# First stage of a 512-token two-block network: half the chunk turns on each partition half, tables copied across, other orders of loads, sines, copies and products

## The chip, the cores and the metric

The kernel runs on one core of a Trainium2 chip. The core has five engines that run side by side, each through its own list of instructions in order: TensorE (PE, matrix products and transposes), VectorE (DVE), ScalarE (ACT), GpSimd (POOL) and SyncE (SP), which here only issues transfers (DMA). They wait for each other through semaphores. The metric is the time of one execution on the device in microseconds (us); lower is better.

## What is computed

A network of a first block (two layers: a diagonal state-space mixer "S5", then sparse attention, each with a gated MLP) and a second block (four kinds of attention, cross attention into 256 memory tokens, an MLP). The change touches only the S5 mixer at the start and the key/value product of the memory tokens that runs beside it:

```python
def s5_mixer(u, lam_re, lam_im, log_dt, b_re, b_im, c_re, c_im, d_skip, w_glu):
    lam = lax.complex(lam_re, lam_im)
    dt = jnp.exp(log_dt)[:, None]
    a_bar = jnp.exp(lam * dt)
    b_bar = ((a_bar - 1.0) / lam)[..., None] * lax.complex(b_re, b_im)
    ug = u.reshape(bsz, length, S5_GROUPS, S5_GROUP)      # 64 groups of 16 channels
    bu = jnp.einsum('blgh,gph->blgp', ug, b_bar)          # 64 complex states per group
    _, states = lax.associative_scan(_ssm_combine, (a_seq, bu), axis=1)
    y = jnp.einsum('blgp,ghp->blgh', states, c).real.reshape(bsz, length, D_MODEL)
    y = y + d_skip * u
    y = jax.nn.gelu(y)
    val, gate = jnp.split(y @ w_glu, 2, axis=-1)
    return val * jax.nn.sigmoid(gate)
```

The input `u` is the RMS-normed `x` (512 tokens of 1024 channels), all in float32.

## The kernel before

The program is one list of instructions for each engine, written out by hand, with semaphores between them. The order on an engine is the order of the code; nothing is scheduled by a tool.

The S5 stage cuts the 512 tokens into 64 chunks of 8 tokens. Inside a chunk the recurrence is a matrix product (the "taps"); from chunk to chunk it is a scan with a real decay, after the states have been turned back by the chunk's angle, and forth again after the scan. For this there are two tables, `tab_c` and `tab_s` (cosine and sine of group times chunk, 128 partitions by 64 groups by 64 chunks). Partitions 0 to 63 hold the real part and 64 to 127 the imaginary part of the same 64 states, so both halves of a table are the same numbers.

Preparation. DVE makes the powers of the transition (`exp_small`, `cmul`), then per block of 8 groups an input map (`input_map(b)`, into `in_w`) and an output map (`output_map(b)`, into `out_a`), and once the angles in turns, reduced to a fraction (`chunk_turns`, three operations over the whole table, lines 1479 to 1481). ACT squares the eight slices of `x` (L799), copies the transposed memory (`memT`, L829), the B and C matrices (`b_s`, `c_n`, `c_s`), scales `x` into `u` (L855, eight slices), and makes the tables (`table(k)`, four quarters, each of a sine, an absolute value and a sine, L890, L891, L893). PE transposes the weights and `u` and computes keys and values of the memory (L2004, L2008).

The loop over eight blocks b of 8 groups. On PE: `s5_rotate_in(b)` (L2060, L2061), `s5_in(b+1)`, `s5_lags(b+1)`, `s5_rotate_out(b)`, `s5_in_turn(b+2)`, `s5_out(b)` (L2018, L2019). On DVE: `rotate_in(b)` (L1518, L1519, the first reader of the tables), `input_map(b+2)`, `scan_chunks(b)`, `output_map(b+2)`. On ACT: `lag_out(b+1)` (L878), `states_out(b)` (L885), `decay_out(b+1)`, `in_map_out(b+2)`, `gelu(b)` (L860). `states_out(b)` feeds `s5_out(b)`. SP copies `lag` to `taps` by eight transfers a block, after `s5_out(b-1)` (semaphore `s5_y`) and `lag_out(b)`; `lag_out(b+1)` waits until the taps of block b have landed, and `s5_out(b)` as well.

Behind the loop comes the gated product with `w_glu` (the GLU, L2121), whose weights pass in slots through `raw`: SP loads a slot by two transfers, ACT rounds it (`round_slot`, L899), POOL makes the rest (`split_rest`, L647). The rounding of slot 0 stands on ACT ahead of the last `states_out`:

```python
            act.wait_ge(s5_v, NB)
            round_slot(0, 0, 1)
            states_out(NB - 1)
```

## Time and profile before

| what | value |
|---|---|
| median of three runs | 1960.52 us (1957.99 to 1961.86) |
| the profiled execution | 1957.8 us |
| its span (first to last instruction) | 1955.9 us |
| granted TensorE clock, mean over the span, as a share of full speed | 0.991 |
| PE busy | 1905.9 us, 97% of the span |
| start of the GLU's matmuls behind the S5 stage | 168.5 us |

The profile gives the start and the length of each instruction, counted from the span's start, and what ended the idle time before it. A matmul's record overlaps the next one, so the distance from one start to the next is its cost. PEclk is the clock granted to TensorE: 1.00 is 2.4 GHz, 0.50 is 1.2 GHz.

### The profile page before, as it was taken

How to read it: one execution, taken by the hardware profiler on the slowest of the kernel's cores; microseconds unless marked ns; L12 is line 12 of the kernel's file. 1: busy time of each engine (PE TensorE's matmuls, PEld its weight loads, DVE VectorE, ACT ScalarE, POOL GpSimd, SP SyncE). 2: the span in 40 equal slices, each digit the busy share in tenths (PEclk: the TensorE clock that was granted, in tenths of full speed). 3: DMA queues.
4: the chain of work that ended last, by engine and by line, in shares of the span. 5: the costliest groups of instructions: out<-in, count | busy, mean ns of one | idle time of the engine just before them, and what ended most of it. 6: DMA issues, size and time to landing. Idle time of an engine off the chain costs nothing.

```text
span 1955.9 us, 24958 instructions
## 1 busy us (share of the span) xinstructions
PE 1905.9 (97%) x9663; PEld 1541.8 (79%) x9663; DVE 749.2 (38%) x1281; ACT 742.2 (38%) x1142; POOL 826.9 (42%) x412
## 2 busy tenths in 40 slices
PE   5999999999999999999999999999999999999998
PEld 4777888888888878767888888888775778888887
DVE  7983231111002378882311110020546657403721
ACT  6634242232223243684423222242457462212212
POOL 1003444444444458654434344444245444343433
PEclk9899999999999899999999999999999999999999
DMA  7114323333322213202333323324220223324231
GB/s 192 27 25 138 99 82 100 93 100 86 103 95 70 83 65 105 68 2 65 87 106 87 105 78 102 115 87 145 76 65 16 83 56 96 108 86 108 86 108 64
DMA packets 209706, 169.26 MB, mean 87 GB/s; under 512 B 19545, under 2 KB 174633, under 8 KB 209560
## 3 DMA queue, kind: packets, MB, share of 16 engines
q1 hardware_dynamic: 207456, 164.61, 28.5%
q10 hardware_dynamic: 2168, 3.52, 0.5%
q8 instruction: 55, 0.90, 0.2%
q14 instruction: 27, 0.22, 0.0%
HBM read 163.10 MB, written 2.65 MB: 85 GB/s over the span
## 4 chain that ended last, share of the span: by engine, by line
PE 89%; ACT 3%; DVE 3%; issue 2%; DMA 1%; POOL 1%; SPq 1%; POOLq 0%; DVEq 0%; ACTq 0%
PE PS L2121 77%; PE PS L2411 2%; PE PS L2402 2%; PE PS L2421 2%; DMA xp<-in_x 1%; PE PS L2018 1%; PE PS L2019 1%; PE PS L2194 1%; DVE taken L1884 1%; PE PS L2364 0%; ACT probs_t L1188 0%; PE PS L2039 0%; SPq L494 0%; PE PS L2051 0%; ACT junk L799 0%
## 5 line engine op out<-in xcount | busy, mean ns | idle before, releaser
L647 POOL TENSOR_TENSOR w_lo<-raw,w_hi 128x2048 fp32r<-128x2048 f32 x145 | 670.5, 4624 | 960.7 <-ACT w_hi L899 837.5
L899 ACT ACTIVATE w_hi<-raw 128x2048 fp32r<-128x2048 f32 x145 | 277.8, 1916 | 629.6 <-PE PS L2121 629.6
L2121 PE MATMUL PS<-xT_hi,w_hi 128*128 128x512 f32 (+1 forms) x1152 | 441.0, 383 | 1.5 <-DVE xT_lo L1568 1.1
L2121 PE MATMUL PS<-xT_lo,w_hi 128*128 128x512 f32 (+1 forms) x1152 | 438.2, 380 | 0.0
L2121 PE MATMUL PS<-xT_hi,w_lo 128*128 128x512 f32 (+1 forms) x1152 | 438.0, 380 | 0.0
L2121 PEld LDWEIGHTS PS<-xT_hi,w_hi 128*128 128x128 f32 x1152 | 216.6, 188 | 47.4 <-issue 6.7
L2121 PEld LDWEIGHTS PS<-xT_lo,w_hi 128*128 128x128 f32 x1152 | 216.6, 188 | 41.5
L2121 PEld LDWEIGHTS PS<-xT_hi,w_lo 128*128 128x128 f32 x1152 | 216.7, 188 | 40.5
L2121 PE MATMUL PS<-w_hi,hT_hi 128*128 128x512 f32 x608 | 236.9, 390 | 0.0
L2121 PE MATMUL PS<-w_hi,hT_lo 128*128 128x512 f32 x608 | 236.6, 389 | 0.0
L2121 PE MATMUL PS<-w_lo,hT_hi 128*128 128x512 f32 x608 | 236.5, 389 | 0.0
L2121 PE MATMUL PS<-w_hi,xT_hi 128*128 128x512 f32 (+2 forms) x592 | 231.9, 392 | 0.7 <-ACT ki_raw L1102 0.7
L2121 PE MATMUL PS<-w_hi,xT_lo 128*128 128x512 f32 (+2 forms) x592 | 228.6, 386 | 0.0
L2121 PE MATMUL PS<-w_lo,xT_hi 128*128 128x512 f32 (+2 forms) x592 | 228.4, 386 | 0.0
L1637 DVE TENSOR_TENSOR x_res<-x_res,PS 128x512 f32<-128x512 f32 x40 | 27.4, 686 | 397.3 <-PE PS L2121 397.3
L1654 DVE TENSOR_TENSOR gbuf<-gbuf,PS 128x512 f32<-128x512 f32 x44 | 30.3, 688 | 378.4 <-PE PS L2121 378.4
L2121 PEld LDWEIGHTS PS<-w_hi,xT_hi 128*128 128x128 f32 x592 | 114.0, 193 | 28.8 <-issue 8.5
L2121 PEld LDWEIGHTS PS<-w_lo,hT_hi 128*128 128x128 f32 x608 | 114.1, 188 | 23.7
L2121 PEld LDWEIGHTS PS<-w_hi,hT_lo 128*128 128x128 f32 x608 | 114.1, 188 | 23.6
L2121 PEld LDWEIGHTS PS<-w_hi,hT_hi 128*128 128x128 f32 x608 | 114.1, 188 | 23.6
L2121 PEld LDWEIGHTS PS<-w_hi,xT_lo 128*128 128x128 f32 x592 | 114.2, 193 | 21.4
L2121 PEld LDWEIGHTS PS<-w_lo,xT_hi 128*128 128x128 f32 x592 | 114.3, 193 | 19.9
(335 smaller groups left out, 2024.7 us busy)
## 6 DMA issues: line engine op xcount, KB each, us to landing
raw<-in_ffn_w_gate_up SPq DMA_DIRECT2D x88, 512.0 KB, 4.5
raw<-in_ffn_w_down SPq DMA_DIRECT2D x40, 512.0 KB, 4.3
raw<-in_w_up SPq DMA_DIRECT2D x32, 512.0 KB, 5.1
raw<-in_w_down SPq DMA_DIRECT2D x32, 512.0 KB, 4.3
raw<-in_dsa_w_in SPq DMA_DIRECT2D x28, 512.0 KB, 4.4
raw<-in_w_in SPq DMA_DIRECT2D x21, 512.0 KB, 4.4
raw<-in_s_w_glu SPq DMA_DIRECT2D x16, 512.0 KB, 4.5
raw<-in_dsa_w_o SPq DMA_DIRECT2D x8, 512.0 KB, 4.7
```

Of the source, the lines that this page charges most:

```text
L647: pool.tensor_tensor(w_lo[:, par, :], raw[:, par, :], f32(w_hi[:, par, :]), ALU.subtract).then_inc(w_split, 1)
L899: act.activation(w_hi[:, par, :], raw[:, par, :], ACT.Copy).then_inc(w_rounded, 1)
L1637: tt(x_res[:, tb, cols], x_res[:, tb, cols], PS[:, 4 + tb, :], ALU.add).then_inc(n_free, 1)
L1654: tt(gbuf[:, pair, 1, :], gbuf[:, pair, 0, :], PS[:, 2 * pair + 1, :], ALU.mult).then_inc(t_free, 1)
L1884: tt(lg[:, :, 0:cols - 1], lg[:, :, 0:cols - 1], rest[:, :, 1:cols], ALU.mult).then_inc(st_prob, 1)
L2018: mm(o, uT[:, GB * b + g, :], taps[:, g, :, :].rearrange("p t h -> p (t h)"), start=True, stop=False)
L2019: ins = mm(o, states[:, g, :], out_a[b % 3][:, g, 1:CH + 1, :].rearrange("p t h -> p (t h)"), start=False, stop=True)
L2121: ins = mm(o, a if weights_stay else c, c if weights_stay else a, start=first and n == 0, stop=last and n == 2)
L2194: ins = tr(PS[:, banks[4 * (tb // 2) + i], at:at + P], x_n[:, tb, P * k:P * k + P], ident[:, :])
L2402: mm(PS[:, dot_bank(u0, t), 0:k.shape[1]], q[half:half + HD], k[half:half + HD], start=True, stop=True).then_inc(col_dot, 1)
L2411: ins = tr(PS[:, 4 + e % 2, P * j:P * j + P], probs[:, e % ring, P * j:P * j + P], ident[:, :])
L2421: ins = mm(PS[HD * i:HD * i + HD, 6 + (p // 4) % 2, at:at + P], units[2 * p + i][3][j], probs_t[:, 2 * (p % 2) + i, P * j:P * j + P], star ...
```

## The change

- The angles in turns are made for half of the groups on each partition half (`turns`, in `raw`, groups 0 to 31 on partitions 0 to 63, the others on 64 to 127). `table(n)` makes a quarter of the tables on one partition half; SP copies it to the other half by two transfers (`table_copy`).
- On ACT `table(0)` stands behind `lag_out(0)`, `table(1)` behind `in_map_out(1)`, `table(2)` behind `lag_out(1)` and `table(3)` behind `lag_out(2)`, the last one behind the first GELU.
- ACT's first activation is a sine; the two small sines stand ahead of the copies of B. The swapped `b_s` is copied after four squares, three squares stand behind `c_s`. The rsqrt of `x` is made in halves. The copy of the keys stands in the middle of the `u` slices.
- The row of `norm_mix` is loaded once (4 KB) and spread over the partitions by a product with ones, where it was loaded 128 times (512 KB). `log_dt` is loaded first, and the first exponential waits for it alone.
- PE makes the swap of B right behind the memory's transposes, and the values in two parts, the second behind `s5_lags(0)`. The transposes of `u` go to the banks in another order.
- Slot 0 of `w_glu` is loaded behind the taps of all eight blocks, where it was loaded behind the keys.

```diff
@@ table of turns
-        turns_i = place("turns_i", "arena", 48 * KB, [P, G, NC], I32)
+        turns_i = place("turns_i", "w_lo", 0, [P, G // 2, NC], I32)
+        turns = place("turns", "raw", 0, [P, G // 2, NC])
@@ SP, the loads
+            sp.dma_start(small[:, 0, :], w["s5_log_dt"][0:1, :].broadcast_to([P, G])).then_inc(ld_dt, 16)
...
-            sp.dma_start(small[:, 0, :], w["s5_log_dt"][0:1, :].broadcast_to([P, G])).then_inc(ld_lam, 16)
+            sp.dma_start(g_row[:, :], w["norm_mix"][0:1, :]).then_inc(ld_rows, 16)
...
-            sp.dma_start(g_row[:, :], w["norm_mix"][0:1, :].broadcast_to([P, D])).then_inc(ld_rows, 16)
@@ SP, the GLU's first slot
-                    else:
-                        sp.wait_ge(kv_done, g + 1)
-                    v = raw[:, g % 2, :].rearrange("p (k t n) -> p k t n", t=2, n=256)
-                    put(g % 2, v[:, :, 0, :], glu[:, k:k + 4, 256 * j:256 * j + 256])
-                    put(g % 2, v[:, :, 1, :], glu[:, k:k + 4, D + 256 * j:D + 256 * j + 256])
                     if g == 0:
+                        def table_copy(n):
+                            side, gs = n // 2, slice(G // TABS * n, G // TABS * n + G // TABS)
+                            of, to = slice(GP * side, GP * side + GP), slice(GP - GP * side, P - GP * side)
+                            sp.wait_ge(s5_cos, 2 * n + 2)
+                            sp.dma_start(tab_s[to, gs, :], tab_s[of, gs, :]).then_inc(s5_tab[n], 16)
+                            sp.dma_start(tab_c[to, gs, :], tab_c[of, gs, :]).then_inc(s5_tab[n], 16)
...
+                            if b == 0:
+                                table_copy(0)
+                                table_copy(1)
+                                sp.wait_ge(kv_sb, 2)
+                                sp.dma_start(kv_dram, kv_new[:, :, :]).then_inc(kv_out, 16)
+                            if b == 1:
+                                table_copy(2)
+                                table_copy(3)
+                    v = raw[:, g % 2, :].rearrange("p (k t n) -> p k t n", t=2, n=256)
+                    put(g % 2, v[:, :, 0, :], glu[:, k:k + 4, 256 * j:256 * j + 256])
+                    put(g % 2, v[:, :, 1, :], glu[:, k:k + 4, D + 256 * j:D + 256 * j + 256])
@@ ACT
-            act.activation(warm[:, :], sign[:, :], ACT.Copy)
+            act.activation(warm[:, :], sign[:, :], ACT.Sin)
...
-            def table(k):
-                gs = slice(G // TABS * k, G // TABS * (k + 1))
+            def table(n):
+                side, at = n // 2, G // TABS * (n % 2)
+                rows, gs, of = slice(GP * side, GP * side + GP), slice(G // TABS * n, G // TABS * n + G // TABS), slice(at, at + G // TABS)
                 act.wait_ge(s5_turns, 1)
...
-            kv_copy(0)
-            kv_copy(1)
             in_map_out(0)
             lag_out(0)
+            table(0)
+            kv_copy(1)
             for q in range(8):
...
             decay_out(0)
-            table(0)
             in_map_out(1)
-            for k in range(1, TABS):
-                table(k)
+            table(1)
             for b in range(NB - 1):
                 lag_out(b + 1)
+                if b < 2:
+                    table(2 + b)
                 states_out(b)
@@ DVE
-            dve.wait_ge(ld_lam, 16 * 5)
+            dve.wait_ge(ld_dt, 16)
+            exp_small(pt(3), pt(0), pt(4), pt(5), pt(6))
             dve.wait_ge(ld_const, 16 * 2)
             dve.wait_ge(s5_nat_sb, 1)
-            exp_small(pt(3), pt(0), pt(4), pt(5), pt(6))
...
                 if b % 2 == 0:
-                    dve.wait_ge(s5_cos, b + 2)
+                    dve.wait_ge(s5_tab[b // 2], 32)
```

Three places show how the lists change. ACT before, from the last quarter of the tables into the loop (y is the GELU's output, ACT_TABLE_LOAD the change of the function tables between sine and GELU):

```order
L890 ACTIVATE tab_s<-tab_c 128x1024
L891 ACTIVATE tab_c<-tab_c 128x1024
L893 ACTIVATE tab_c<-tab_c,quarter 128x1024
L878 ACTIVATE lag<-PS 16x1024
L885 ACTIVATE states<-PS 128x512
L866 ACTIVATE decay<-r 128x8x63
L872 ACTIVATE in_t<-PS 128x1024
L860 ACT_TABLE_LOAD
L860 ACTIVATE y<-PS 64x8x8x16
L878 ACTIVATE lag<-PS 16x1024
L885 ACTIVATE states<-PS 128x512
```

ACT of the change, from the same `lag_out(1)` on:

```order
L899 ACTIVATE lag<-PS 16x1024
L914 ACTIVATE tab_s<-turns 64x1024
L915 ACTIVATE turns<-turns 64x1024
L917 ACTIVATE tab_c<-turns,quarter 64x1024
L906 ACTIVATE states<-PS 128x512
L887 ACTIVATE decay<-r 128x8x63
L893 ACTIVATE in_t<-PS 128x1024
L881 ACT_TABLE_LOAD
L881 ACTIVATE y<-PS 64x8x8x16
L899 ACTIVATE lag<-PS 16x1024
L914 ACT_TABLE_LOAD
L914 ACTIVATE tab_s<-turns 64x1024
```

Before, no table work stands between `lag` and `states`. Now a quarter stands there in blocks 0 and 1, the second one with a change of function tables ahead; its other two operations and then `states` follow.

SP before, with the waits, from the first load of `w_glu` on:

```order
L454 DMA raw<-in_s_w_glu 128x4x256 [waits kv_done]
L454 DMA raw<-in_s_w_glu 128x4x256
L487 DMA kv_dram<-kv_new 128x1024 [waits kv_sb]
L494 DMA taps<-lag 16x1024 [waits s5_lag_sb,s5_zero]
L494 DMA taps<-lag 16x8x112
L494 DMA taps<-lag 16x8x96
```

SP of the change, the same place and then the end of the last block's taps:

```order
L499 DMA taps<-lag 16x8x32
L499 DMA taps<-lag 16x8x16
L490 DMA tab_s<-tab_s 64x1024 [waits s5_cos]
L491 DMA tab_c<-tab_c 64x1024
L490 DMA tab_s<-tab_s 64x1024 [waits s5_cos]
L491 DMA tab_c<-tab_c 64x1024
L505 DMA kv_dram<-kv_new 128x1024 [waits kv_sb]
```

```order
L499 DMA taps<-lag 16x8x64
L499 DMA taps<-lag 16x8x48
L499 DMA taps<-lag 16x8x32
L499 DMA taps<-lag 16x8x16
L458 DMA raw<-in_s_w_glu 128x4x256 x4
L515 DMA x_res<-in_x 128x4x1024 [waits s5_gelu]
```

The load of slot 0 has moved from ahead of the first taps to behind the last ones, where it now stands together with slot 1 (four transfers); the first table copies stand behind the eight taps transfers of block 0.

## Rows read from the trace of the kernel before

**Rows 1.** The page, part 1: busy time by engine.

```profile
PE 1905.9 (97%) x9663; PEld 1541.8 (79%) x9663; DVE 749.2 (38%) x1281; ACT 742.2 (38%) x1142; POOL 826.9 (42%) x412
```

**Rows 2.** Timeline of DVE up to the loop: start, us, what, idle before.

```profile
8.19 0.20 DVE L1391 TENSOR_SCALAR small<-small 128x64 f32<-128x64 f32 x1 [5.55 <-ACT small L802]
...
18.47 0.22 DVE L1416 TENSOR_TENSOR small<-small 128x64 f32<-128x64 f32 x1 [1.62 <-ACT small L812]
...
47.33 4.42 DVE L1479 TENSOR_TENSOR tab_c<-small,rot 128x4096 f32<-128x4096 f32 x1 [0.24 <-ACT u L855]
...
54.12 4.42 DVE L1481 TENSOR_TENSOR tab_c<-tab_c,turns_i 128x4096 f32<-128x4096 f32 x1
...
66.57 0.69 DVE L1518 TENSOR_TENSOR v<-PS,tab_c 128x512 f32<-128x512 f32 x1
```

**Rows 3.** Timeline of ACT up to the loop.

```profile
16.74 1.28 ACT L811 ACT_TABLE_LOAD   x1
...
24.18 1.06 ACT L799 ACTIVATE junk<-xp 64x1024 f32<-64x1024 f32 x1 [1.60 <-DMA xp<-in_x]
...
38.87 8.43 ACT L855 ACTIVATE u<-xp,rstd 64x1024 f32<-64x1024 f32 x8
...
60.77 1.05 ACT L890 ACTIVATE tab_s<-tab_c 128x1024 f32<-128x1024 f32 x1
...
62.79 1.15 ACT L893 ACTIVATE tab_c<-tab_c,quarter 128x1024 f32<-128x1024 f32 x1
```

**Rows 4.** SP's issues and their landing: the taps (64 issues) and `kv_dram`.

```profile
L494 SPq DMA_DIRECT2D taps<-lag x64: 559/600/1822, 53.7 to 160.9; - x64
DMA to landing us min/median/max: 1.8/2.2/3.4
...
kv_dram<-kv_new SPq DMA_DIRECT2D x1, 512.0 KB, 2.7
```

**Rows 5.** Timeline of PE in the loop's blocks 0 and 1.

```profile
67.92 2.07 PE L2060 MATMUL PS<-v,ident 128*128 128x512 f32 x2 [2.12 <-DVE v L1519]
...
78.61 0.43 PE L2018 MATMUL PS<-taps,uT 128*64 128x128 f32 x2
...
82.25 1.12 PE L2060 MATMUL PS<-v,ident 128*128 128x512 f32 x2
...
90.75 0.43 PE L2018 MATMUL PS<-taps,uT 128*64 128x128 f32 x2
```

**Rows 6.** Timeline of ACT in block 1.

```profile
88.76 1.01 ACT L878 ACTIVATE lag<-PS 16x1024 f32<-16x1024 f32 x1 [5.39 <-DMA taps<-lag]
89.99 0.60 ACT L885 ACTIVATE states<-PS 128x512 f32<-128x512 f32 x1 [0.21 <-PE PS L2069]
```

**Rows 7.** Timeline of ACT, SP and PE at the end of the loop.

```profile
156.37 1.02 ACT L860 ACTIVATE y<-PS 64x1024 f32<-64x1024 f32 x1 [4.25 <-PE PS L2019]
157.29 1.90 ACT L899 ACTIVATE w_hi<-raw 128x2048 fp32r<-128x2048 f32 x1
159.94 0.60 ACT L885 ACTIVATE states<-PS 128x512 f32<-128x512 f32 x1 [0.75 <-PE PS L2069]
...
161.52 1.14 SPq L454 DMA_DIRECT2D raw<-in_s_w_glu  x2
...
162.76 0.40 PE L2018 MATMUL PS<-taps,uT 128*64 128x128 f32 x2 [2.22 <-issue]
...
166.37 2.23 PE L2097 MATMUL PS<-ident,y 64*128 64x64 f32 x32
168.53 0.50 PE L2121 MATMUL PS<-w_hi,xT_hi 128*128 128x512 f32 x1
```

**Rows 8.** What the transfers moved from 161.4 to 167.0 us, in 40 slices.

```profile
GB/s 14 75 29 0 0 39 20 0 0 0 102 146 168 256 366 300 366 329 307 380 395 329 366 351 380 373 380 388 380 388 395 293 205 117 29 0 0 0 0 0
```

**Rows 9.** Stretches of PE: us, length, busy (x), PEclk, DMA share, GB/s.

```profile
55.00:55.50 0.50, 0.50 (x11) 0.83 0.61 98
...
72.00:72.50 0.50, 0.50 (x5) 0.61 0.00 0
...
1948.00:1949.00 1.00, 0.88 (x4) 1.00 0.06 25
...
1953.00:1954.00 1.00, 0.00 (x0) 0.57 0.29 115
```

More of the change, by code:

```diff
@@ L39 @@
 TABS = 4
+TURN_BANKS = [4, 5, 6, 0, 1, 2, 3, 7]
 HD = 64
@@ L640, in _ @@
             rsqrt(rstd[:, 32:34], ssq[:, 32:34], 2, 1.0 / D).then_inc(mem_rstd, 1)
-            pool.wait_ge(s5_sq, CH)
-            rsqrt(rstd[0:NC, 0:CH], ssq[0:NC, 0:CH], CH, 1.0 / D, NC).then_inc(s5_rstd, 1)
+            for half in range(2):
+                rows = slice(CH // 2 * half, CH // 2 * half + CH // 2)
+                pool.wait_ge(s5_sq, rows.stop)
+                rsqrt(rstd[0:NC, rows], ssq[0:NC, rows], CH // 2, 1.0 / D, NC).then_inc(s5_rstd, 1)
             def split_rest(g, par):
@@ L802, in _ @@
             act.activation(small[:, 1:3, :].rearrange("p a g -> p (a g)"), PS[:, 0, 0:2 * G], ACT.Copy).then_inc(s5_nat_sb, 1)
+            act.wait_ge(s5_ang, 1)
+            act.activation(small[:, 12, :], small[:, 11, :], ACT.Sin).then_inc(s5_sin, 1)
+            act.activation(small[:, 13, :], small[:, 11, :], ACT.Sin, scale=0.5).then_inc(s5_sin, 1)
             act.wait_ge(s5_nat, 2)
@@ L1472, in _ @@
             link(ts(pt(5).bitcast(I32), pt(11), cycles, None, ALU.mult))
-            link(stt(pt(10), pt(5).bitcast(I32), -1.0, pt(10), ALU.mult, ALU.add))
+            for side in range(2):
+                rows, gs = slice(GP * side, GP * side + GP), slice(G // 2 * side, G // 2 * side + G // 2)
+                link(stt(small[rows, 13, 0:G // 2], small[rows, 5, gs].bitcast(I32), -1.0, small[rows, 10, gs], ALU.mult, ALU.add))
             def chunk_turns():
-                dve.wait_ge(s5_u, CH)
+                dve.wait_ge(kv_done, 1)
                 dve.wait_ge(ld_rot, 16)
-                link(tt(tab_c[:, :, :], pt(10).unsqueeze(2).broadcast_to([P, G, NC]), rot[:, 3 * P:3 * P + NC].unsqueeze(1).broadcast_to([P, G, NC]), ALU.mult))
-                link(ts(turns_i[:, :, :], tab_c[:, :, :], 1.0, None, ALU.mult))
-                tt(tab_c[:, :, :], tab_c[:, :, :], turns_i[:, :, :], ALU.subtract).then_inc(s5_turns, 1)
+                link(tt(turns[:, :, :], small[:, 13, 0:G // 2].unsqueeze(2).broadcast_to([P, G // 2, NC]),
+                        rot[:, 3 * P:3 * P + NC].unsqueeze(1).broadcast_to([P, G // 2, NC]), ALU.mult))
+                link(ts(turns_i[:, :, :], turns[:, :, :], 1.0, None, ALU.mult))
+                tt(turns[:, :, :], turns[:, :, :], turns_i[:, :, :], ALU.subtract).then_inc(s5_turns, 1)
             def over_k(ap, b, n):
@@ L1975, in _ @@
             tr(PS[:, 0, 0:len(GAINS) * KT], gain_rows[:, :], ident[0:len(GAINS) * KT, 0:len(GAINS) * KT]).then_inc(gains_t, 1)
+            pe.wait_ge(ld_rows, 16)
+            pe.wait_ge(const_set, 1)
+            for b in range(2):
+                ins = mm(PS[:, 5 + b, :], ones[0:1, :], g_row[:, 512 * b:512 * b + 512], start=True, stop=True)
+            ins.then_inc(s5_grow, 1)
             pe.wait_ge(s5_nat_sb, 3)
@@ L1983, in _ @@
                     ins.then_inc(mem_t, 1)
+            pe.wait_ge(s5_bn, 1)
+            pe.wait_ge(ld_rot, 16)
+            pe.wait_ge(gains_sb, 1)
+            for b in range(2):
+                ins = mm(PS[:, 7 * b, :], rot[:, 2 * P:3 * P], b_n[:, 32 * b:32 * b + 32, :].rearrange("p g h -> p (g h)"), start=True, stop=True)
+            ins.then_inc(s5_swap, 1)
             pe.wait_ge(ld_c, 16 * 3)
```

106 lines of the change are left out of this document (52 added, 54 removed).

## The prediction

> **What bounds the kernel now.** I read the page first. PE is busy for 97% of the span [rows 1], and behind the first stage nothing in the lists changes; so the question is when PE starts the GLU's matmuls, 168.5 us before [rows 7], and everything behind moves with that. Then I read the timelines of the first stage engine by engine. Up to the loop the start is set by ACT and DVE in turn: `x` lands at 24.2, ACT then works without a pause until the last slice of `u` at 47.3 (38.87 + 8.43) [rows 3], only then may DVE make the turns, which take from 47.33 to 58.54, and after the two maps of block 1 it reaches the first `rotate_in` at 66.57 [rows 2]. The loop is bound by PE: one round, from 67.92 on, has matmuls back to back, and rounds are about 12.2 us long (78.61 to 90.75) [rows 5]. But PE waits for ACT's `states` at the end of each round, and ACT reaches it only just in time: in block 1 `lag` waits for the taps' landing, starts at 88.76, and `states` starts 0.2 us behind its end [rows 6]. So anything put between `lag` and `states` lands on the path. The loop's end is also tight: slot 0 is rounded at 157.29, long after its load, `states` follows at 159.94, and the last `s5_out` starts at 162.76 when the last taps land [rows 7].
>
> **Part 1, up to the loop.** `x` is issued behind one small transfer more (0.6 us), and the 512 KB broadcast stood behind it in the queue; I take its landing as 0.3 us later. From there to the end of `u` ACT has the same work as before (23.1 us, 24.18 to 47.30) plus one copy of 512 columns (0.6, as `states` [rows 6]) in the middle: 24.5 + 23.7 = 48.2. I see no wait in it, since the swap on PE stands earlier than before. Then `in_map_out(0)` and `lag_out(0)`, 1.0 each as `lag` [rows 6]: 50.1. `table(0)` has 1024 elements a partition as before, only on 64 partitions; a quarter took 3.17 (60.77 to 63.94) [rows 3]. If time goes by elements per partition it is 3.2 again, and it ends at 53.3. Halving the partitions gains ACT nothing.
>
> DVE gains twice. The first exponential (fourteen operations of about 0.25, 3.5 us) now fits into the 5.55 us in which DVE waited, and the 1.62 us wait for the small sines loses the table load of 1.28 [rows 2, 3]: about 4.6 us together. So the first input and output maps end near 42 instead of 47.1, the turns cost half of 11.2 (5.6) and end at 47.7, and the maps of block 1 (58.54 to 66.57 before, 8.0 with two small memsets) end at 55.7 [rows 2]. All of this is ahead of ACT, so DVE waits.
>
> SP issues the eight taps transfers of block 0 behind `lag`, from 50.1, 0.64 us each: 55.2. Then the two copies of `table(0)`, 256 KB each, the second issued at 55.8. No such copy is in the trace. The nearest row is `kv_dram`, 512 KB from SBUF in 2.7 us [rows 4]; from below the shortest taps landing, 1.8, from above the 4.5 us of a loaded slot (161.5 to 166.0) [rows 8]. I take 2.9, nearest to `kv_dram`: the table is there at 58.7, and `rotate_in(0)` starts at about 58.8 where it was 66.57. **Minus 7.8** (bounds -8.9 and -6.2). PE has its part (`u`, `s5_in(0)`) done by 58 even at half clock.
>
> **Part 2, the first two rounds.** From `rotate_in(0)` on DVE to `s5_out(0)` on PE it took 12.0 us (66.57 to 78.61), part of it at 1.2 GHz: the clock fell at 55.3 in the narrow transposes of `u` and rose at 72.2, 4.3 us after PE went back to work at 67.92 [rows 5, 9]. I keep that, so PE is ready at 70.9. Its `lags` of this round end near 68.2; `lag_out(1)` takes 1.0, and then `table(2)` stands ahead of `states_out(0)`: 3.15 + 0.6, so `states` is there at 72.9. Before, the tables were all made by then. **Plus 2.0** (0.5 to 3.2).
>
> In round 1 `table(3)` stands between `lag_out(2)` and `states_out(1)`, behind the first GELU, so the function tables must change back: 1.28 + 3.17 = 4.45 [rows 3]. The slack was 0.2 us [rows 6]. PE needs nothing else and idles: **plus 4.2** (3.1 if the load could run ahead of the wait for `lag`, 4.5 at most). The load back for `gelu(1)` (1.28) lies in ACT's wait for `s5_out(1)`, which is 2 us in every round. `table_copy(2)` and `(3)` are issued behind the taps of block 1 and have two rounds before `rotate_in(4)`: nothing.
>
> The row gives 1.28 us for a change of tables (16.74), and DVE waited 1.62 for it with a sine behind it [rows 2, 3]. The Trainium skill, "ScalarE: Activation LUTs", section "What ACT_TABLE_LOAD costs", counts a drain on top and says about 2.66 us for every switch; by that the sum below would be 1.4 higher. No gap for such a drain stands in this trace ahead of the load, so the rows decide.
>
> After round 1 the loop stands at -7.8 + 2.0 + 4.2 = -1.6. Rounds 2 to 6 are as before.
>
> **Part 3, the loop's end.** Call T the time when `s5_out(6)` is done, 156.3 before [rows 7]. The last taps are issued from T to T + 5.2, then slot 0. Before, the two transfers issued there (slot 1, 161.52) had landed at 166.0, which is T + 9.7 [rows 7, 8]. Now slot 0 has that place. ACT meets `round_slot(0)` ahead of `states_out(7)`, and cannot pass it: T + 9.8, + 1.9 for rounding, + 0.6 for `states`, so the last `s5_out` starts at T + 12.3 instead of T + 6.4. **Plus 5.9** (4.9 with a landing 1 us sooner; 8.9 if slots 0 and 1, now issued together, share the bandwidth). Behind this `s5_out` stand on PE the turns of `y` and the GLU; POOL's split of slot 0 (4.6 us, beside `s5_out`) and slot 1 are ready before PE asks.
>
> PE idles about 8.4 us there. At the end of the trace the clock fell to 0.50 at 1953.1, 4.3 us after the last matmul at 1948.9 [rows 9]; an idle time of 2.2 us ahead of 162.76 cost nothing. So PE resumes at 1.2 GHz, and if it needs 4.3 us again, half of that is lost: **plus 2.1** (0 if it stays high; 5.8 if `s5_out` and the turns, 3.6 + 2.2 us, run wholly at half speed).
>
> **Sum.** -7.8 + 2.0 + 4.2 + 5.9 + 2.1 = +6.4 us. The profiled execution took 1957.8 (span 1955.9), so its counterpart is 1964.2. It lies 2.7 below the median of the runs; against the median 1960.5 I predict **1966.9**. A difference under 0.2% (3.9 us) can't be told from no change.
>
> **Rivals.**
> - *The clock stays at 2.4 GHz.* If PE's denser work before 60 us keeps the clock up, `s5_out(0)` comes 2.2 us earlier (half of the 4.3 us), and if the idle time at the end doesn't lower it, 2.1 more: +2.1, 1962.6, not to be told from no change. For it: PE now works with fewer pauses before the loop. Against it: the narrow transposes of `u`, in which it fell, are still there, and an idle time of 4.3 us did lower it. It decides at both places together. Chance 0.13.
> - *More is lost.* The 4.1 us idle time in round 1 is as long as the one after which the clock fell, which would cost another 2.1; or slot 0 lands with slot 1, up to 3.0. +8.5 to +9.5, about 1969.5. Chance 0.17. The Trainium skill, "TensorE: Matmul & The Clock Gate", Part 1, lets the clock fall after an idle stretch and rise only after sustained work, which speaks for this rival; the trace agrees at its end.
> - *`x` lands earlier.* If the broadcast took bandwidth from `x` (B, the memory and `x` are 3.9 MB from about 7 to 24.2 us, so 512 KB are 2.3 us by this estimate), everything on ACT up to the loop moves by 2.6: +3.8, 1964.3. Against it: it was issued behind `x`. Chance 0.09.
> - *Faster.* The copies land in 1.8 us, `x` earlier, and the clock high: -1.0 or less. It needs all three. Chance 0.04.
>
> **How the numbers follow.** The forecast has 0.57, its own range +4 to +9 (1964.5 to 1969.5). Slower by over 0.2%: nearly all of it and the second rival, and half of the third, 0.79. Within 0.2%: the first rival, half of the third and the forecast's edge, 0.16. Faster 0.05. The range 1962.0 to 1971.0 takes in the first two rivals.
>
> **What would show it.** `rotate_in(0)` on DVE near 58.8, released by a transfer; a PE wait of 2 us ahead of `s5_out(0)` and of 4 us ahead of `s5_out(1)`, both for ACT's `states`; a table load inside round 1 of 1.28; the rounding of slot 0 at about 164.5, released by a transfer, and the last `s5_out` at 167, with a granted clock of 0.50; the GLU at about 175 instead of 168.5. The prediction is wrong if slot 0 lands much earlier or later than T + 9.7, or if the loop starts more than 1.5 us away from 60.

## The result, and the profile after

The changed kernel takes **1968.57 us** (median of six runs, 1967.32 to 1970.75); the kernel before, run beside it on the same chip, takes 1958.01 us (median of six, 1957.37 to 1961.86). The ratio is 1.0052, with a 95% interval of 1.0039 to 1.0065: slower by 10.6 us. The profiled execution took 1967.32 us (span 1965.5), 9.5 more than the one of before; the difference of the spans is 9.6, and that is what the following rows account for. The page's busy times hardly differ from those of before [rows 1]: PE's is 4.9 higher, DVE's 5.8 lower (the turns over half the elements). So what is lost has to be looked for in PE's waits and in the clock.

```profile
PE 1910.8 (97%) x9667; PEld 1544.9 (79%) x9667; DVE 743.4 (38%) x1282; ACT 742.7 (38%) x1143; POOL 829.1 (42%) x414
```

**Up to the loop.** Timeline of the changed kernel (start, length, what, idle time before it and what ended it): ACT's first slice of `x`, then SP's issues, then DVE's first reader of the tables.

```profile
23.95 1.06 ACT L817 ACTIVATE junk<-xp 64x1024 f32<-64x1024 f32 x1 [3.06 <-DMA xp<-in_x]
...
49.44 5.58 SPq L499 DMA_DIRECT2D taps<-lag  x8
55.06 0.60 SPq L490 DMA_DIRECT2D tab_s<-tab_s  x1
55.70 0.60 SPq L491 DMA_DIRECT2D tab_c<-tab_c  x1
...
59.36 0.69 DVE L1546 TENSOR_TENSOR v<-PS,tab_c 128x512 f32<-128x512 f32 x1 [4.02 <-DMA tab_c<-tab_c]
```

`rotate_in(0)` starts at 59.36 where it was 66.57 [rows 2]: 7.2 us sooner. DVE had nothing to do for 4.02 us there; it was released by the copy of `tab_c` across the partitions, issued at 55.70 behind the eight taps transfers. The copies took this long from issue to landing (minimum, median and maximum of the four of `tab_c`; `tab_s` had 2.9, 2.9 and 3.0):

```profile
DMA to landing us min/median/max: 3.5/3.6/4.0
```

**The first two rounds.** ACT's timeline, then PE's.

```profile
67.94 1.02 ACT L899 ACTIVATE lag<-PS 16x1024 f32<-16x1024 f32 x1 [4.67 <-PE PS L2078]
68.98 1.06 ACT L914 ACTIVATE tab_s<-turns 64x1024 f32<-64x1024 f32 x1
...
72.18 0.60 ACT L906 ACTIVATE states<-PS 128x512 f32<-128x512 f32 x1
...
84.73 1.01 ACT L899 ACTIVATE lag<-PS 16x1024 f32<-16x1024 f32 x1 [5.47 <-DMA taps<-lag]
85.76 1.28 ACT L914 ACT_TABLE_LOAD   x1
87.06 1.05 ACT L914 ACTIVATE tab_s<-turns 64x1024 f32<-64x1024 f32 x1
...
90.25 0.60 ACT L906 ACTIVATE states<-PS 128x512 f32<-128x512 f32 x1
```

```profile
72.83 0.43 PE L2054 MATMUL PS<-taps,uT 128*64 128x128 f32 x2 [2.14 <-ACT states L906]
...
78.14 1.13 PE L2096 MATMUL PS<-v,ident 128*128 128x512 f32 x2
90.90 0.69 PE L2054 MATMUL PS<-taps,uT 128*64 128x128 f32 x2 [4.19 <-ACT states L906]
...
96.18 1.12 PE L2096 MATMUL PS<-v,ident 128*128 128x512 f32 x2
```

Both tables lie between `lag` and `states`, and PE waits for `states` 2.14 and 4.19 us. What the reader should also see are the distances behind these waits: `s5_out(0)` takes 72.83 to 78.14, 5.31 us, and `s5_out(1)` 90.90 to 96.18, 5.28 us, where it took 3.64 before (78.61 to 82.25 [rows 5]). Nothing was added to it; the granted clock is low (below).

**The loop's end.** SP, ACT and PE in the changed kernel.

```profile
158.69 5.08 SPq L499 DMA_DIRECT2D taps<-lag  x8
163.81 2.24 SPq L458 DMA_DIRECT2D raw<-in_s_w_glu  x4
...
158.65 1.02 ACT L881 ACTIVATE y<-PS 64x1024 f32<-64x1024 f32 x1 [4.25 <-PE PS L2055]
169.52 1.91 ACT L923 ACTIVATE w_hi<-raw 128x2048 fp32r<-128x2048 f32 x1 [9.85 <-DMA raw<-in_s_w_glu]
171.34 0.58 ACT L906 ACTIVATE states<-PS 128x512 f32<-128x512 f32 x1
...
171.97 0.69 PE L2054 MATMUL PS<-taps,uT 128*64 128x128 f32 x2 [9.14 <-ACT states L906]
...
177.66 2.23 PE L2135 MATMUL PS<-ident,y 64*128 64x64 f32 x32
179.83 0.50 PE L2159 MATMUL PS<-w_hi,xT_hi 128*128 128x512 f32 x1
```

The four transfers of slots 0 and 1 are issued together behind the last taps, the rounding waits 9.85 us for the first of them, `states` stands behind the rounding, and PE waits 9.14 us. The last `s5_out` takes 5.69 us in place of 3.61 [rows 7], and the GLU starts at 179.83, 11.3 us later than before.

**The clock.** Stretches of PE: start and end, length, busy us of the five engines (instructions), PEclk, DMA share, GB/s. The first six are the changed kernel, where the clock falls and rises (the third and the fourth lie in `s5_out(0)` and `s5_out(1)`); the last stands much later, in the index products of the sparse attention, which the change does not touch.

```profile
53.00:54.00 1.00, 1.00 (x9) 0.88 (x10) 0.96 (x2) 1.00 (x3) 0.00 (x0) 0.67 0.37 63
63.00:64.00 1.00, 1.00 (x4) 0.34 (x2) 0.96 (x2) 0.27 (x1) 0.00 (x0) 0.71 0.00 0
...
74.00:75.00 1.00, 1.00 (x7) 1.00 (x6) 0.97 (x2) 0.98 (x2) 0.00 (x0) 0.50 0.00 0
92.00:93.00 1.00, 1.00 (x7) 1.00 (x6) 0.00 (x0) 0.98 (x2) 0.00 (x0) 0.50 1.08 229
...
166.00:167.00 1.00, 0.00 (x0) 0.00 (x0) 0.00 (x0) 0.00 (x0) 0.00 (x0) 0.50 1.00 340
176.00:177.00 1.00, 1.00 (x10) 1.00 (x9) 1.00 (x2) 0.00 (x0) 0.16 (x1) 0.89 0.00 0
...
665.00:677.00 12.00, 11.35 (x50) 10.87 (x50) 0.51 (x2) 2.42 (x3) 2.85 (x4) 0.50 0.29 89
```

And the same place in the kernel before:

```profile
653.00:669.00 16.00, 15.35 (x61) 14.21 (x61) 3.10 (x4) 2.63 (x3) 6.47 (x5) 0.50 0.21 67
```

The late stretch at 1.2 GHz is 3.4 us shorter in the changed kernel's profile (13.7 with its ends, in place of 17.1). The first row behind the GLU that both have (a square of `x_res`) is at 263.31 and at 252.01, still 11.3 apart; at the end of the span it is 9.6. So 1.7 of the loss is given back in that stretch. The term belongs to this execution and not to the change: a second profile of the same program (below) has 20.5 there.

### The profile page after: what moved, and what is told of

It is laid out like the page before. It is cut to its first block, busy times and chain, and to the rows that moved or that the text cites. A ratio compares the mean times of both kernels' runs of the same rounds, so it can differ in the third digit from the quotient of the medians.

```text
span 1965.5 us, 24986 instructions
## 1 busy us (share of the span) xinstructions
PE 1910.8 (97%) x9667; PEld 1544.9 (79%) x9667; DVE 743.4 (38%) x1282; ACT 742.7 (38%) x1143; POOL 829.1 (42%) x414
## 4 chain that ended last, share of the span: by engine, by line
PE 88%; ACT 4%; DVE 2%; issue 2%; DMA 2%; SPq 2%; POOL 1%; POOLq 0%; DVEq 0%; ACTq 0%
PE PS L2159 77%; PE PS L2449 2%; PE PS L2440 2%; PE PS L2459 2%; SPq L499 1%; PE PS L2054 1%; DMA xp<-in_x 1%; PE PS L2055 1%; PE PS L2232 1%; DVE taken L1911 1%; PE PS L2402 0%; PE PS L2383 0%; ACT probs_t L1212 0%; ACT junk L817 0%; PE PS L2075 0%
```

## The experiments

Each kernel was run beside the kernel before on the same chip; ratios are to that, with 95% intervals. The kernel before took 1958.4, 1958.3 and 1958.4 us (medians) in the three sessions. "Changed" is the kernel under study.

| kernel | median us (runs) | ratio to before |
|---|---|---|
| changed, again | 1968.65 (5) | 1.0052 (1.0038 to 1.0066) |
| slot 0 early | 1960.96 (11) | 1.0019 (1.0010 to 1.0028) |
| rounding behind `states` | 1968.61 (5) | 1.0066 (1.0052 to 1.0080) |
| tables 2 and 3 moved | 1959.69 (11) | 1.0007 (0.9998 to 1.0016) |
| both | 1951.62 (6) | 0.9967 (0.9955 to 0.9979) |
| PE kept busy | 1963.43 (10) | 1.0025 (1.0015 to 1.0034) |
| turns late | 1970.85 (5) | 1.0056 (1.0042 to 1.0070) |
| both, copies first | 1949.02 (5) | 0.9950 (0.9936 to 0.9963) |
| broadcast as before | 1968.76 (5) | 1.0050 (1.0037 to 1.0064) |
| both, whole turns | 1955.00 (11) | 0.9983 (0.9974 to 0.9992) |

The theory was that of the prediction (the late slot 0, and the tables between `lag` and `states`), with the clock's fall behind each of the waits added once the profile had shown it. The rivals were that one of them is only order and not time, that the clock falls for another reason, and that the start of the loop hangs on something else.

### Slot 0 loaded early

```diff
+            def glu_load(g, j, k):
+                v = raw[:, g % 2, :].rearrange("p (k t n) -> p k t n", t=2, n=256)
+                put(g % 2, v[:, :, 0, :], glu[:, k:k + 4, 256 * j:256 * j + 256])
+                put(g % 2, v[:, :, 1, :], glu[:, k:k + 4, D + 256 * j:D + 256 * j + 256])
...
                             if b == 1:
                                 table_copy(2)
                                 table_copy(3)
-                    v = raw[:, g % 2, :].rearrange("p (k t n) -> p k t n", t=2, n=256)
-                    put(g % 2, v[:, :, 0, :], glu[:, k:k + 4, 256 * j:256 * j + 256])
-                    put(g % 2, v[:, :, 1, :], glu[:, k:k + 4, D + 256 * j:D + 256 * j + 256])
+                                glu_load(g, j, k)
+                    else:
+                        glu_load(g, j, k)
```

> The changed kernel with one thing undone: the load of slot 0 of w_glu is issued behind the copies of the rotation's tables (in round 1) and not behind the last block's taps. Everything else as changed. Theory of the prediction: raw has landed long before w_hi wants it, so ACT's wait of 9.85 us ahead of w_hi goes, states follows gelu at once, PE's stall of 9.14 us ahead of the last s5_out falls to about 2, and the last s5_out starts some 7.0 us sooner; with the stall short, the clock stays at full speed there and s5_out takes 3.64 again in place of 5.7: another 2.1. The GLU's first product starts at about 170.5 in place of 179.83, and the kernel takes about 1959.5 (9 less than changed, within 1 to 2 of before). Rival 1, the load would only collide with the taps of the early rounds: then rotate_in of blocks 2 or 3 starts late and 2 to 4 of the 9 are given back: 1962 to 1964. Rival 2, the clock's fall at the end doesn't follow from the idle time but from the narrow transposes ahead of it: then s5_out still takes 5.7 and the gain is 7: 1961.5.

Measured 1960.96, 7.6 less than changed. ACT no longer waits for `raw`, and the last `s5_out` starts at 165.33. The profile of this kernel on PE:

```profile
165.33 0.40 PE L2061 MATMUL PS<-taps,uT 128*64 128x128 f32 x2 [2.25 <-issue]
...
170.60 2.23 PE L2142 MATMUL PS<-ident,y 64*128 64x64 f32 x32
172.76 0.50 PE L2166 MATMUL PS<-w_hi,xT_hi 128*128 128x512 f32 x1
```

The wait and the 6.6 us that hung on it are gone (171.97 to 165.33). But this `s5_out` takes 5.27 us, so the clock is low here too, behind 2.25 us of idle time that cost nothing before: the second term, 2.1, came back by only 0.4 in this execution. The GLU starts 7.1 sooner. That is the number of the second rival. Its reason (the narrow transposes ahead) is not borne out: the kernel before and the next one have the same transposes and the same idle time and keep their clock there, and the kernel that was kept busy (below) has seven wide matmuls between the transposes and the wait and loses it. The first rival falls: rounds 2 and 3 are as in the changed kernel.

### The rounding of slot 0 behind the last `states`

```diff
-            act.wait_ge(s5_v, NB)
-            round_slot(0, 0, 1)
             states_out(NB - 1)
...
             gelu(NB - 1)
+            act.wait_ge(s5_v, NB)
+            round_slot(0, 0, 1)
```

> The changed kernel with the load of slot 0 left where it is, but ACT's rounding of slot 0 moved from ahead of the last block's states to behind its second gelu. It parts the late load into its two effects: that states waits behind a rounding which waits for the load, and that the GLU itself waits for the split slot. Theory of the prediction: states follows the maps at once, the last s5_out starts about 7 us sooner (near 165) with a stall of about 2 in place of 9.14, and its clock stays full. The GLU's first product then waits for slot 0: raw lands about 169.5, w_hi takes 1.9 and POOL's split 4.6 behind it, so about 176 in place of 179.83, or, where the split can follow w_hi closely, 174: the kernel takes about 1965 to 1963 (3.5 to 5.5 less than changed). Rival, that only the order on ACT mattered: the GLU starts at about 170.5 and the kernel takes about 1959.5. Rival, that the order on ACT didn't matter: no change, 1968.5.

Measured 1968.61: nothing gained. This expectation failed by 3.6 us and more, and the third possibility named came true in the number, though the order did change where PE waits. PE in this kernel:

```profile
165.53 0.40 PE L2054 MATMUL PS<-taps,uT 128*64 128x128 f32 x2 [2.25 <-issue]
...
169.14 2.23 PE L2135 MATMUL PS<-ident,y 64*128 64x64 f32 x32
176.90 0.80 PE L2159 MATMUL PS<-w_hi,xT_hi 128*128 128x512 f32 x1 [5.52 <-POOL w_lo L665]
```

```profile
174.00:178.00 4.00, 1.10 (x3) 0.91 (x4) 3.27 (x4) 3.61 (x4) 3.16 (x2) 0.55 0.85 347
178.00:182.00 4.00, 4.00 (x13) 3.15 (x12) 0.00 (x0) 0.00 (x0) 4.00 (x1) 0.60 0.81 269
```

Up to the last `s5_out` all goes as said: it starts at 165.53, behind the same 2.25 us of idle time as in the kernel above, and takes 3.61 us, at full clock. Then PE waits 5.52 us for POOL's split of the late slot; the GLU starts at 176.90, 2.9 sooner than in the changed kernel, but at 1.2 GHz. At the square of `x_res` it is 0.9 ahead (262.38 against 263.31): 2.0 were lost to the clock. The rest went with the late stretch of the index products, from 662 to 680 here, 17.1 us in place of 13.7. So even without these two, no more than 2.9 us hung on the order in this profile, where the early load takes 7.1 off. The lateness of the slot is the main cause in itself; the order on ACT decides above all where PE waits for it.

### Tables 2 and 3 moved

```diff
             in_map_out(1)
             table(1)
+            table(2)
             for b in range(NB - 1):
                 lag_out(b + 1)
-                if b < 2:
-                    table(2 + b)
                 states_out(b)
                 decay_out(b + 1)
                 if b + 2 < NB:
                     in_map_out(b + 2)
+                if b == 0:
+                    table(3)
```

> The changed kernel with the load of slot 0 left late, and the two tables that stood between a block's lag products and its states moved: table(2) right behind table(1), ahead of the lag of block 1, and table(3) behind the maps of block 2, ahead of the first gelu, so that no load of a function table is added. Theory of the prediction: PE's stalls ahead of s5_out(0) and s5_out(1) (2.14 and 4.19 us) go, that is 2.1 and 4.2; and as I now read the trace of the changed kernel, the half clock behind each of these stalls (s5_out 5.3 us in place of 3.64, twice) goes with them: 1.65 and 1.65 more. In all 9.6, less what the moved tables cost where they now stand (their 3.2 us each lie in waits of ACT of 4.67 us and more in block 0; up to 2 us where they don't fit): 1959 to 1961. Rival 1, the half clock in rounds 0 and 1 follows from something else than the stalls: the gain is 6.3 at most: about 1962. Rival 2, the copies of the tables to the other half are the limit and not ACT: less than 3 are gained, 1966 or more.

Measured 1959.69, 8.9 less than changed, in the range given. PE runs into `s5_out(0)` and `s5_out(1)` without a wait, and both take 3.6 us again:

```profile
70.86 0.43 PE L2055 MATMUL PS<-taps,uT 128*64 128x128 f32 x2
...
74.49 1.13 PE L2097 MATMUL PS<-v,ident 128*128 128x512 f32 x2
...
83.00 0.43 PE L2055 MATMUL PS<-taps,uT 128*64 128x128 f32 x2
...
86.64 1.12 PE L2097 MATMUL PS<-v,ident 128*128 128x512 f32 x2
```

So two tables of 3.2 us each cost nothing where ACT had waited anyway (`lag_out(1)` still waits 1.85 us behind `table(2)`), and 6.3 us (2.1 + 4.2) plus the clock where they stood. Both rivals fall.

### Both

This kernel has the edits of "slot 0 early" and of "tables 2 and 3 moved", and nothing else.

> The two edits together: slot 0 of w_glu loaded early and tables 2 and 3 moved off the way of states. What remains of the change is the shorter preparation with its 7.2 us before block 0. Theory of the prediction: 7.0 + 2.1 and 6.3 + 3.3 come off the changed kernel, less up to 2 for the tables where they now stand: 1968.6 - 9.1 - 7.6 to 9.6 = 1950 to 1952, some 6 to 8 under before. Rival, that the time before the loop is eaten by a later wait anyway (the loop ends when something else allows it): 1956 to 1959, about as before. Rival, that the later stretches at half clock move against it (the one in the index products was 4.1 us shorter in the changed kernel's profile): 1952 to 1954.

Measured 1951.62, 17.0 less than changed; the two gains alone are 7.6 and 8.9, and add up to 16.5. It is 6.8 us (0.3%) faster than the kernel before. What is left of the change, the shorter preparation, is worth by the medians about what it brings forward the loop (59.74 in place of 66.57). The profile of this kernel doesn't show it place by place: it is its slowest execution, PE runs at 1.2 GHz from 53.3 to 70.3 us, the last `s5_out` takes 5.28, and the GLU starts at 166.01, only 2.5 sooner than before.

### The changed kernel again, and PE kept busy

The first has no edit. The second adds matmuls without a use, 2, 3 and 7 of them, ahead of `s5_out(0)`, `s5_out(1)` and the last one:

```diff
+            def keep_busy(n, half):
+                for _ in range(n):
+                    mm(PS[:, 6 + half, :], ident[:, :], cz[:, :, :].rearrange("p g c -> p (g c)"), start=True, stop=True)
...
+                if b == 0:
+                    keep_busy(2, 0)
+                if b == 1:
+                    pe.wait_ge(s5_gelu, 1)
+                    keep_busy(3, 0)
                 s5_out(b)
...
+            pe.wait_ge(s5_gelu, NB - 1)
+            keep_busy(7, 1)
             s5_out(NB - 1)
```

> The changed kernel itself once more, on this chip, beside the next three. Expected 1968.5 (1967 to 1971). It also gives a second profile of the same program: in the profiles so far the stretches at 1.2 GHz stand at other places from kernel to kernel where the waits are alike (behind the 2.14 us stall of round 0 the clock fell in two kernels and not in a third). If the place is settled by the program, this profile has them at 53 to 64, 73 to 78, 90 to 95, 165 to 177 and 664 to 678 us again; if not, at least one of the short ones is missing or longer, and the run's time differs by half of that.

> The changed kernel with matmuls added on PE whose result nobody reads: 2 ahead of s5_out(0), 3 ahead of s5_out(1) and 7 ahead of the last s5_out, each 128x512 and about 1.0 us, in time that PE otherwise waits there (2.14, 4.19 and 9.14 us). Nothing else moves. Theory: the clock falls because PE idles, so it stays at 2.4 GHz at these three places and each s5_out takes 3.64 us again: 1.65 + 1.65 + 2.1 less, 1963 (1962 to 1965). Rival, the fall follows from how narrow the matmuls of s5_out are and not from the idle time: the stretches at 1.2 GHz stay, and the time stays at 1968.5. Rival, the added matmuls get in the way of the waits: up to 1 us more.

The same program gave 1968.65 again. Its second profile (an execution of 1971.04) differs in the clock alone: behind the 2.14 us wait of round 0 the clock stays high (1.00 in each row from 72 to 76 us), in round 1 it falls before PE has resumed and `s5_out(1)` takes 6.45 us, the last `s5_out` takes 6.57, and the late stretch is longer, 19 us and its ends where it was 12. Second profile of the changed kernel:

```profile
73.00:74.00 1.00, 0.41 (x4) 0.41 (x5) 0.97 (x2) 0.98 (x2) 0.00 (x0) 1.00 0.00 0
...
89.00:90.00 1.00, 0.01 (x1) 0.01 (x1) 0.97 (x2) 0.95 (x3) 0.00 (x0) 0.50 0.00 0
...
663.00:682.00 19.00, 18.35 (x77) 17.36 (x77) 2.47 (x4) 2.62 (x3) 7.61 (x5) 0.50 0.18 56
```

So where exactly the clock falls is not set by the program. The Trainium skill, "TensorE: Matmul & The Clock Gate", Part 1, says that the moment isn't tied to a kernel's start and differs from run to run; the two profiles agree with that (a fall at 73.8 in one, none in that round in the other).

With PE kept busy the kernel takes 1963.43, 5.1 to 5.2 less, where 5.4 was expected. PE in that kernel:

```profile
70.66 1.88 PE L2141 MATMUL PS<-cz,ident 128*128 128x512 f32 x4
72.96 0.43 PE L2054 MATMUL PS<-taps,uT 128*64 128x128 f32 x2 [0.42 <-ACT states L906]
...
89.34 0.43 PE L2054 MATMUL PS<-taps,uT 128*64 128x128 f32 x2 [1.59 <-ACT states L906]
...
168.42 0.43 PE L2054 MATMUL PS<-taps,uT 128*64 128x128 f32 x2 [2.94 <-ACT states L906]
```

The clock is 1.00 through both early `s5_out`, which take 3.6 us again, behind waits for `states` that are as long as before but partly filled. So the rival (the narrow matmuls of `s5_out`) falls, and the clock by itself cost 3.3 us there in the profile of the changed kernel (2.8 in its second one, all of it in round 1). At the end only part of the theory held: 2.94 us were left idle, and the last `s5_out` still takes 5.31 us (168.42 to 173.73). In the profile the GLU starts 3.95 us sooner than in the changed kernel (175.88), and the span is 4.1 shorter; the other 1.1 between the medians this one profile doesn't show.

### DVE's turns held back

```diff
             def chunk_turns():
                 dve.wait_ge(kv_done, 1)
+                dve.wait_ge(s5_u, CH)
```

> The changed kernel with DVE's turns of block 0 held back until the last slice of u is done (about 47.4 in place of 41.5 us), which asks whether the order of DVE's work or the way of the tables over SP sets the start of the loop. DVE then has nothing to do from 41.5 to 47.4 (5.9 us), its turns end at 53.2 in place of 47.3, and table(0) comes behind them: 53.2 + 3.2 = 56.4, copies landed by about 60.5 at the earliest, as the maps of block 1 end 5.9 us later too, at 61.1. Theory: rotate_in(0) starts at about 61.3 to 62 in place of 59.36, 2 to 2.5 later, and the kernel takes 1971. Rival, other work fills: no change, 1968.5. Rival, everything behind DVE moves by the whole hold: 1974.

Measured 1970.85, where 1971 was expected; but two of the five runs took 1967.8, and the interval overlaps that of the changed kernel, so the time alone doesn't show a loss. The trace does. Turns that wait for the last slice of `u` start at 47.72 behind 6.16 us of nothing, and `rotate_in(0)` starts at 62.16, no longer behind a transfer (the copy of `tab_c`, issued at 57.41, lands within 4.0 us).

```profile
62.16 0.69 DVE L1547 TENSOR_TENSOR v<-PS,tab_c 128x512 f32<-128x512 f32 x1 [0.57 <-DVE sz L1576]
```

DVE's own work ends at 61.59. The 0.57 us behind it end with PE's `s5_in(0)`, which `rotate_in(0)` reads as well: PE runs it from 58.39 to 62.06, late since PE had waited 4.94 us for the copy of the values, which stands on ACT behind the now late `table(0)`. So of the 6.2 us that DVE wins by making the turns in other memory, ahead of the end of `u`, at most 2.8 reach the loop; the wait for the copies swallows the rest.

### Copies ahead of the taps

This is the kernel of "both" with one thing more.

```diff
                         sp.wait_ge(s5_zero, 1)
+                        table_copy(0)
                         for b in range(NB):
                             sp.wait_ge(s5_lag_sb, b + 1)
...
                             if b == 0:
-                                table_copy(0)
                                 table_copy(1)
```

> The version with slot 0 loaded early and tables 2 and 3 moved (1951.6), and with one thing more: SP issues the copies of table 0 to the other half of the partitions ahead of the eight issues of taps of block 0 (5.9 us on SP). In that version DVE stood 4.44 us ahead of rotate_in(0) for tab_c, whose copy was issued at 56.08 and landed at 59.7; table 0 is ready at 52.4. Theory: both copies go out by 53.6, land by about 57, and rotate_in(0) starts at about 57.2 in place of 59.74: 2.5 less; but PE's maps end only at 59.2 there and must be ahead of rotate_in on PE, so that PE saves 1.8, its stall: 1949.8 (1949 to 1950.5). Rival, the taps come too late for block 0's lag products or s5_out: nothing gained, 1951.6, or up to 1 worse.

Measured 1949.02, 2.6 less than "both" and 9.2 us (0.5%) faster than the kernel before: the best version. The intervals of the two ratios just overlap (to 0.9963 here, from 0.9955 there), but no run of this kernel is as slow as the fastest of "both" (1950.51 and 1950.58). The copies are issued 3.2 us earlier, and DVE waits 1.66 us in place of 4.44:

```profile
52.35 0.51 SPq L497 DMA_DIRECT2D tab_s<-tab_s  x1
52.90 0.60 SPq L498 DMA_DIRECT2D tab_c<-tab_c  x1
...
56.98 0.69 DVE L1554 TENSOR_TENSOR v<-PS,tab_c 128x512 f32<-128x512 f32 x1 [1.66 <-DMA tab_c<-tab_c]
```

I had thought that PE's maps would hold `rotate_in(0)` on PE until 59.2; it came at 58.41, right behind them. The taps, now later, keep nobody waiting in that round.

### The broadcast as before

```diff
-            sp.dma_start(g_row[:, :], w["norm_mix"][0:1, :]).then_inc(ld_rows, 16)
...
             sp.dma_start(xp[:, :, :], w["x"].rearrange("(c s) d -> c s d", s=CH)).then_inc(ld_x, 16)
+            sp.dma_start(g_row[:, :], w["norm_mix"][0:1, :].broadcast_to([P, D])).then_inc(ld_rows, 16)
...
-                ins = mm(PS[:, 5 + b, :], ones[0:1, :], g_row[:, 512 * b:512 * b + 512], start=True, stop=True)
```

> The changed kernel with the row norm_mix fetched as before: a broadcast of 512 KB to 128 partitions, issued behind x, and without the 4 KB row ahead of x and PE's two products with ones. Theory: x was ahead of the broadcast in the queue either way, so it lands within 0.3 us of the changed kernel's 23.95, the first u and with it the start of the loop stay, and the kernel takes 1968.5 (1967.5 to 1969.5). Rival (the third of the prediction): the broadcast takes bandwidth from x, which lands up to 2.3 us later, and the start of the loop and the kernel move by as much, to about 1970.8. Rival: DVE now waits for a row that lands behind x, and the swap with all that follows is late: 1970 or more.

Measured 1968.76: no difference. `x` is there at 23.68 in place of 23.95, so a broadcast issued behind it takes nothing from it. DVE's turns are 1.45 us later (42.92), and the wait for `tab_c`, now 2.98, hides most of it: `rotate_in(0)` starts at 59.77 in place of 59.36.

### Whole turns

This too is "both" with one thing more: the turns and tables are made on all partitions, and nothing is copied across.

```diff
-                            sp.dma_start(tab_s[to, gs, :], tab_s[of, gs, :]).then_inc(s5_tab[n], 16)
-                            sp.dma_start(tab_c[to, gs, :], tab_c[of, gs, :]).then_inc(s5_tab[n], 16)
...
-                link(tt(turns[:, :, :], small[:, 13, 0:G // 2].unsqueeze(2).broadcast_to([P, G // 2, NC]),
-                        rot[:, 3 * P:3 * P + NC].unsqueeze(1).broadcast_to([P, G // 2, NC]), ALU.mult))
+                for half, at in enumerate((turns[:, :, :], tab_c[:, G // 2:G, :])):
+                    if half:
+                        dve.wait_ge(s5_u, CH)
+                        dve.wait_ge(s5_turns, 1)
+                    link(tt(at, small[:, 10, G // 2 * half:G // 2 * half + G // 2].unsqueeze(2).broadcast_to([P, G // 2, NC]),
+                            rot[:, 3 * P:3 * P + NC].unsqueeze(1).broadcast_to([P, G // 2, NC]), ALU.mult))
```

> The version with slot 0 early and tables 2 and 3 moved (1951.6), and with the half turns undone: DVE makes the turns of all 64 groups on all 128 partitions, in two pieces of 32 groups (5.8 us each, the second from 47.5 to 53.3), the tables are made on 128 partitions, and nothing is copied across. It prices what the halves are worth by themselves. Theory: DVE ends the maps of block 1 near 61.2 in place of 55.2, and no transfer is waited for, so rotate_in(0) starts at 61.3 in place of 59.74: 1.5 more, 1953.1 (1952 to 1954); against the version with the copies issued first (1949.0) the halves are worth some 4. Rival: the loop's start is set by PE at half clock (its maps of block 1 end at 59.2 and move with DVE's), so that more than 1.5 is lost: 1955. Rival: the missing copies and issues of SP free something: 1951.6 or less.

Measured 1955.00, 3.4 more than "both". `rotate_in(0)` starts at 62.30, behind DVE's own work, where "both" had 59.74; 0.8 of it is that `u` was done later in this execution. The first theory's range (to 1954) was missed by 1.0, and the intervals of the two ratios leave both 1.5 and 3.4 open; they overlap by a little, so the sign is only just clear of the noise. The single profiles are no help: here the GLU starts at 165.17, 0.8 sooner than in "both", since the clock was low for 13.7 us around the loop's start in place of 17.1 and stayed up in the last `s5_out`. By the medians, doing half the turns on each partition half and copying them across is worth some 2 to 3 us as the change has it, and about 6 with the copies issued first. What the other orders ahead of the loop (the sines, the swap, the rsqrt in halves) are worth one by one no run shows.

## Why the prediction was right, and where not

The prediction was 1966.9 (1962.0 to 1971.0), slower with a chance of 0.79; measured were 1968.57 and slower. Each term beside its measurement, in the spans of the two profiled executions:

| term | predicted | measured |
|---|---|---|
| start of the loop | -7.8 | -7.2 (66.57 to 59.36) |
| clock from there to `s5_out(0)` | 0 | -0.7 (13.47 us, of them 2.14 waiting, against 12.04) |
| `table(2)` ahead of `states(0)` | +2.0 | +2.1 |
| low clock in `s5_out(0)` | 0 | +1.7 (5.31 against 3.64) |
| `table(3)` and its load in round 1 | +4.2 | +4.3 |
| low clock in `s5_out(1)` | 0 | +1.6 (5.28 against 3.64) |
| rounds 2 to 6 | 0 | +0.5 (waits for `states` of 0.39 and 0.28) |
| slot 0 behind the last taps | +5.9 | +6.9 |
| low clock in the last `s5_out` | +2.1 | +2.1 (5.69 against 3.61) |
| start of the GLU | +6.4 | +11.3 |
| late stretch in the index products | 0 | -1.7 |
| span | +6.4 | +9.6 |

**The mechanisms were right.** Each wait stands where it was said, with the engine that was said, and three of the four sizes are within 0.6 us. That the late slot and the tables cause the loss is shown: moving the tables takes 8.9 us off, the early slot 7.6, both 17.0. Two readings of the prediction are slightly off, without weight for the sum: the row of 72.0 to 72.5 [rows 9], with 0.61, puts the clock's rise at 72.4 and not 72.2, and the idle time at the end is 8.1 by its own terms (2.2 + 5.9) where it says 8.4; measured were 9.14.

**The table load.** The row of before (1.28) decided against the higher price. The profile has 1.28 (85.76) with the sine 0.02 us behind its end and nothing ahead of it, and the whole wait came out at 4.19. The Trainium skill, "ScalarE: Activation LUTs", section "What ACT_TABLE_LOAD costs", would have it 1.4 longer; no run here shows that.

**The landing of slot 0 was mis-sized.** Predicted T + 9.7 by the transfers of slot 1 alone [rows 7, 8], measured T + 10.9 (158.65 to 169.52, T taken at `gelu`'s start). The second rival had the reason, that the two slots are issued together and share what the transfers can move, with up to 3.0; it was 1. The trace speaks for it: from 165.0 to 169.5 the transfers moved 1.3 MB (290 GB/s), and slot 0 is 1.05, so part of slot 1 came ahead of slot 0's end. No run issues slot 0 alone at that place, so this is read and not tested.

**The clock was the step that failed.** Part 3 charged it at the end. Part 2 put it at nothing in rounds 0 and 1: for round 0 the one row that bears on it is the idle time of 2.2 us ahead of 162.76, which cost nothing [rows 7]; for round 1, where 4.2 us of idle time were forecast, it gives no reason, and names the fall only as a rival. The row of before was one execution, and it was luck: behind an idle time of 2.1 to 2.3 us the clock fell in four of six profiles in round 0 (2.14 us) and in three of six at the loop's end (2.22 to 2.25 us, the profile of before among those where it didn't). Behind waits of 4.2 us and longer it fell in every one. The second rival charged 2.1 for the fall in round 1; it was 1.6 there and 1.7 in round 0, and 2.8 and nothing in the second profile of the same program. That PE's idling does it in the first two rounds, and not its narrow work, two things show: of the seven profiles with `table(3)` in round 1, only that of the kernel that was kept busy has a high clock there, and in the four kernels with the tables moved, where PE has no wait in these rounds, the clock stayed high in both `s5_out`. Why 2.2 us of idle time lower it in one execution and not in the next, the runs leave open.

**Why the number was near all the same.** That was luck, twice. At the start of the GLU the terms were 4.9 us too low; 1.7 came back in the late stretch, by that one execution, which left 3.2 in the span. And the prediction was made against a median of 1960.5, of three runs, where 22, 14 and 15 later runs gave 1958.3 to 1958.4; that put some 2.2 us back. Against its own profiled execution the forecast was 1964.2, and that execution took 1967.32. So the forecast was 1.7 off, and its working 3.1. The range held the outcome; what the clock does in the first two rounds was missing from the working all the same.

**The rivals.** "The clock stays at 2.4 GHz" fell at every place. "More is lost" came true in both of its parts, each at a part of its price; with 0.17 it was given too little. "`x` lands earlier" fell: 0.2 us, and no more with the broadcast back. "Faster" fell.

## What to carry to other kernels

Before work is put between two steps of an engine, look at the slack of the second step in the trace (0.2 us here, ACT's `states`) and at where the same engine waits: two tables cost 8.9 us in the one place and next to nothing about 6 and 15 us earlier, in waits. A load that moves in a queue behind the work of a loop is late by its whole landing, and the other order on ACT that was tried here did not get that back in the time. And price each new wait of TensorE with the clock: behind about 2 us of idle time it fell in 7 of 12 cases, behind 4 us and more in all 12, and each fall made the `s5_out` behind it 1.6 to 3.0 us longer.

## What the runs showed that I had not expected

- The clock can fall after PE has already resumed. In the changed kernel PE stood still until 72.83, and its record slows at about 74; the idle time is over when its price is paid.
- Two executions of one program, 1967.32 and 1971.04 us, differ by the length of a stretch at 1.2 GHz in a stage with matmuls back to back (PE busy 18.35 of 19 us): 13.7 against 20.5 us, half of which difference is most of the 3.7 us between them. Among all the profiles this stretch was between 13.7 and 20.5 us, and the one around the loop's start between 3.4 and 17.1, so single executions of this program can't be compared below some 3 us.
- A copy of a quarter of a table from one partition half to the other (256 KB, 64 partitions) took 2.9 to 4.0 us to land in the changed kernel, more than `kv_dram`'s 512 KB in the kernel before (2.7 [rows 4]). And `kv_dram` itself, now issued while the copies of `table(1)` are under way, took 4.6.
- Half the partitions take ACT as long as all of them: 1.04 us for a sine of 64x1024, 1.05 for 128x1024 [rows 3]. The change gains on DVE since it halves the elements in each partition, on all 128 of them: 2.28 us for the first operation of the turns, where it was 4.42 [rows 2].
